# The order of 32 experts, made on the chip: the two with fewest tokens among the first 128 take the last two places

## The chip, the cores and the metric

The kernel runs on one core of a Trainium2 chip. The metric is device time in microseconds (us), from a launch to its end; lower is better. Engines are named as in the profile: PE is TensorE, DVE VectorE, ACT ScalarE, POOL GpSimd, SP SyncE, the queue that issues most DMAs.

## What is computed

The program computes one layer of a streaming encoder on 512 frames of width 1024, in float32: a norm, attention and a gated DeltaNet side by side, an output projection with a residual, and then a mixture of experts. The change is in the last part. Cut to what matters:

```python
logits = (ht @ router_w) + router_b              # 512 x 32
top_val, top_idx = lax.top_k(logits, TOP_K)      # TOP_K = 4
gates = softmax(top_val)
# each expert e works on the tokens that chose it:
gu  = xb @ w_gu[e] + b_gu[e]                     # 1024 x 2048
act = (clip(gu[:, D_FF:]) + 1) * gate * sigmoid(gate * ALPHA)
yb  = act @ w_down[e] + b_down[e]                # 1024 x 1024
y[token] += yb * gate_of_token
```

Which expert comes first is free, as each adds its part to the output. On these inputs the router of the reference gives the 32 experts this many tokens of all 512, in order of expert: 51 74 60 71 53 46 70 62 83 62 78 78 51 97 91 80 72 31 69 65 77 52 44 38 54 50 73 106 40 44 66 60. Among the first 128 tokens alone: 8 13 14 24 17 11 26 16 19 16 18 17 14 24 26 22 13 10 13 23 16 13 10 11 11 14 11 25 4 13 21 19.

## The kernel before

Everything up to the router runs in the first 340 us. Then the kernel makes lists: the tokens of each expert are cut into blocks of up to 32 (`BT`), an expert with 33 to 64 tokens has two blocks, and all blocks are numbered through. The counts above give 81 blocks; the experts 0 to 31 have 2 3 2 3 2 2 3 2 3 2 3 3 2 4 3 3 3 1 3 3 3 2 2 2 2 2 3 4 2 2 3 2 of them. `LASTB[e]` is the number of expert e's last block. Before the change expert e is worked on at position e.

Weights are loaded whole, 12 MB per expert in six transfers of 2 MB: four for gate and up (`gu_part`, L215), two for down (`dn_part`, L221), and then two small ones for the biases (`biases`, L208 and L210). There are two buffers, `GUW` and `DNW` with index 0 and 1, for even and odd positions. The experts of positions 0 and 1 are loaded early; from position 2 on the loop `reload` on SP does it. SP takes its orders strictly in turn:

- gate-up part q of position p waits (L215) until the last block of position p-2 has read part q of that buffer;
- the down parts wait (L221) for the last block's down product of p-2, which PE does after the first gate-up of position p-1;
- the biases wait for `y_free` (L208), which DVE gives in the first block of position p-1, after its own biases have arrived.

For each block PE does gate-up (L1001, 64 matmul records in the trace) and then down (L1014) of the block before. DVE adds the bias (L1386), clamps, transposes the next block's tokens into `XT` (L1377), and so on. POOL gathers the tokens of a block from memory by indirect DMA (L394; its queue is q0) and adds each finished block to the output (L409). The gather of a block starts when the block before it has been transposed, so there is one in flight. PE's next gate-up needs `XT`. At the first block of a position DVE first waits for the position's biases (L1401), and the transpose of the second block stands behind that wait.

The router: for each of four tiles of 128 tokens, `top4(t)` on DVE (L1306 to L1314) finds the four largest logits and makes the one-hot table `OH` and the counts per token `MASK`. It is put between the additions of the output projection (L1321, two for each tile, numbered n = 0 to 7 here), and PE runs projection, transposes and logits of neighbouring tiles in between (L636, L924). `COUNT` (L636) sums the masks over all 512 tokens; from it come the lists.

Of the kernel before, what the change touches and what calls it, by code (L numbers as in the profile page):

```python
# [36 lines left out]
def hybrid_block(nc, x, norm_mix_w, w_in, qn_w, kn_w, sinks, conv_w, a_log, dt_bias, out_norm_w, w_out,  # L37
                 norm_ffn_w, router_w, router_b, w_gu, b_gu, w_dn, b_dn, out):
    ctx = ExitStack()
    with ctx:  # L40
# [3 lines left out]
        def S_(name):  # L44
            if name not in sems:
                sems[name] = ctx.enter_context(nc.semaphore(name))
            return sems[name]
# [21 lines left out]
        def small(at, n):  # L69
            return SM[:, at:at + n]  # L70
# [92 lines left out]
        NBI = RT[:, 1388:1420].bitcast(I32)  # L163
        GSUM, GREC = RT[:, 1420:1424], RT[:, 1424:1428]
# [19 lines left out]
        COUNT = PS[7][:, 0:NE]  # L184
# [21 lines left out]
        def _(sp):  # L206
# [95 lines left out]
            def reload(e, p):  # L302
                through = sp.value_load(LASTB[0:1, bass.ds(e - 2, 1)], min_val=0, max_val=MAXB - 1) + 1
                gu_part(e, p, range(4), through)
                dn_part(e, p, range(2), through)
                sp.wait_ge(S_("y_free"), e - 1)
                biases(e, p)
# [7 lines left out]
        def _(g):  # L315
# [64 lines left out]
            g.wait_ge(S_("mask"), 2)  # L380
            g.tensor_tensor(MSUM[:, 0, :], MASK[:, 0, :], MASK[:, 1, :], ALU.add).then_inc(S_("msum"), 1)
            normed_out(3)
            g.wait_ge(S_("mask"), 3)
# [250 lines left out]
        def _(pe):  # L634
            def mm(o, l, r, st, sp_):
                return pe.matmul(o, l, r, start=st, stop=sp_)  # L636
# [296 lines left out]
            for n in range(2 * NT):  # L933
                t, half = n // 2, n % 2
                if half == 0:
                    pe.wait_ge(S_("dcat"), t + 1)
                if n == 0:
                    pe.wait_ge(S_("wo_in"), 16 * 3)
                    pe.wait_ge(S_("h_att"), 2 * NT)
                if n >= 2:  # L940
                    pe.wait_ge(S_("h_add"), n - 1)
                for k in range(4, KD):
                    last = mm(PS[n % 2], CAT[:, k, t * P:(t + 1) * P], WO1[:, k - 4, half * 512:half * 512 + 512], k == 4, k == KD - 1)
                last.then_inc(S_("outproj"), 1)
                if n < NT - 1:
                    dcat(n + 1)
                if n in (3, 4, 6):
                    h_transposes(n // 2 - 1)
                if n == 4:
                    pe.wait_ge(S_("rw_scaled"), 1)  # L950
                    logits(0)
                if n == 5:
                    logits(1)
# [17 lines left out]
            pe.wait_ge(S_("mask"), NT)  # L971
# [77 lines left out]
        def _(v):  # L1049
# [254 lines left out]
            def top4(t):  # L1304
                v.wait_ge(S_("lg_ps"), t + 1)
                stt(out=LG[:, t, :], in0=LGP[t % 2], scalar=RSH[:, t:t + 1], in1=RB, op0=ALU.mult, op1=ALU.add).then_inc(S_("logits"), 1)  # L1306
                v.wait_ge(S_("logits"), t + 1)
                link(v.max(MX8[:, t, :], LG[:, t, :]))
                link(v.max_index(MI8[:, t, :], MX8[:, t, :], LG[:, t, :]))
                link(v.tensor_copy(MIF[:, t, :], MI8[:, t, :]))  # L1310
                ts(GATE[:, 4 * t:4 * t + 4], MX8[:, t, 0:4], MX8[:, t, 0:1], None, ALU.subtract).then_inc(S_("v_gate"), 1)
                v.wait_ge(S_("consts"), 8)
                link(tt(OH[:, t], bm(IO32, TOPK), bc(MIF[:, t, 0:TOPK], NE), ALU.is_equal))
                v.tensor_reduce(MASK[:, t, :], OH[:, t].rearrange("p k e -> p e k"), AX.X, ALU.add).then_inc(S_("mask"), 1)  # L1314
            def normed(t):
                stt(out=HN[t], in0=H[t], scalar=RSH[:, t:t + 1], in1=FW, op0=ALU.mult, op1=ALU.mult).then_inc(S_("hn_ready"), 1)
            for t in range(NT):
                for half in range(2):
# [3 lines left out]
                    if half == 0 and t >= 2:  # L1322
                        top4(t - 2)
                    if half == 0 and t == 3:
# [13 lines left out]
            v.wait_ge(S_("count_ps"), 1)  # L1338
# [7 lines left out]
            v.wait_ge(S_("mask"), NT)  # L1346
# [108 lines left out]
```

## Time and profile before

| | |
|---|---|
| median of 3 runs | 1371.28 us (1369.92 to 1372.37) |
| the profiled execution: its time, its span | 1371.59 us, 1369.8 us |
| mean granted TensorE clock | 0.943 of full speed |
| PE busy | 1210.8 us, 88% of the span |
| DVE, POOL, ACT busy | 504.8, 283.8, 206.3 us |
| weight queue (q1) | 424.97 MB, 75.1% of 16 engines' span |
| gathers and scatters (q0) | 18.91 MB, 6.1% |

The span is cut into 40 slices of 34 us, counted here from 0. The row for DMA has the mean busy share of the 16 DMA engines in tenths, the row for GB/s what they moved. From slice 10 on, where the experts begin, the DMA engines are at 9 in all but one slice, while PE moves between 7 and 9. So neither is the only bound: which of the two waits for the other changes along the way, and the averages don't tell it. Times below are in us from the start of the span.

### The profile page before, as it was taken

How to read it: one execution, taken by the hardware profiler on the slowest of the kernel's cores; microseconds unless marked ns; L12 is line 12 of the kernel's file. 1: busy time of each engine (PE TensorE's matmuls, PEld its weight loads, DVE VectorE, ACT ScalarE, POOL GpSimd, SP SyncE). 2: the span in 40 equal slices, each digit the busy share in tenths (PEclk: the TensorE clock that was granted, in tenths of full speed). 3: DMA queues.
4: the chain of work that ended last, by engine and by line, in shares of the span. 5: the costliest groups of instructions: out<-in, count | busy, mean ns of one | idle time of the engine just before them, and what ended most of it. 6: DMA issues, size and time to landing. Idle time of an engine off the chain costs nothing.

```text
span 1369.8 us, 30476 instructions
## 1 busy us (share of the span) xinstructions
PE 1210.8 (88%) x12030; PEld 566.0 (41%) x12031; DVE 504.8 (37%) x1213; ACT 206.3 (15%) x415; POOL 283.8 (21%) x381
## 2 busy tenths in 40 slices
PE   7989997989889887979798899988989777799896
PEld 6865554766533332324233333333333222233333
DVE  1236857455333332323233233323333223233332
ACT  4135662133000000000000000000000000000000
POOL 1000004000122222223122223222222222222222
PEclk9999999899799999989899999999999988999999
DMA  6221140439789999999999999999999999998991
GB/s 204 64 67 62 31 123 8 152 147 397 312 346 415 418 419 415 417 419 416 416 417 419 399 381 395 406 403 417 417 421 418 416 421 419 421 415 353 421 408 27
DMA packets 67696, 446.55 MB, mean 326 GB/s; under 512 B 17008, under 2 KB 37688, under 8 KB 43088
## 3 DMA queue, kind: packets, MB, share of 16 engines
q1 hardware_dynamic: 48736, 424.97, 75.1%
q0 software_dynamic: 16176, 18.91, 6.1%
q10 hardware_dynamic: 2752, 2.23, 0.5%
q8 instruction: 22, 0.36, 0.1%
q14 instruction: 10, 0.08, 0.0%
HBM read 435.37 MB, written 15.07 MB: 329 GB/s over the span
## 4 chain that ended last, share of the span: by engine, by line
DMA 46%; PE 37%; DVE 7%; issue 5%; ACT 1%; POOL 1%; SPq 1%; DVEq 1%; POOLq 1%; ACTq 0%
DMA XG<-hn_scratch,IDXC 22%; DMA BDN<-in_expert_b_down 21%; PE PS L636 17%; PE PS L1001 12%; PE PS L1014 4%; DMA out<-Y,IDXS 3%; PE PSC L636 2%; DVE XT L1377 2%; POOL IDXC L391 1%; DVE GU L1386 1%; DMA W<-in_w_in 1%; SPq L208 1%; DVEq L1423 0%; DVE W L1230 0%; DVE W L1231 0%
## 5 line engine op out<-in xcount | busy, mean ns | idle before, releaser
L1001 PE MATMUL PS<-W,XT 128*32 128x512 f32 x5184 | 608.6, 623 | 116.4 <-DVE XT L1377 107.1
L1001 PEld LDWEIGHTS PS<-W,XT 128*32 128x32 f32 x5184 | 169.3, 114 | 516.5 <-issue 409.0
L1014 PE MATMUL PS<-W,AT 128*32 128x256 f32 x5184 | 294.6, 379 | 1.2 <-DVE AT L1397 1.2
L636 PE MATMUL PS<-W 128*128 128x512 f32 (+7 forms) x898 | 250.2, 439 | 10.4 <-DVE W L1175 7.5
L1014 PEld LDWEIGHTS PS<-W,AT 128*32 128x32 f32 x5184 | 169.5, 110 | 145.8 <-issue 47.8
L636 PEld LDWEIGHTS PS<-W 128*128 128x128 f32 (+1 forms) x898 | 151.8, 195 | 95.0 <-issue 75.3
L1386 DVE TENSOR_TENSOR GU<-PS,BGU 128x512 f32<-128x512 f32 x81 | 56.0, 692 | 363.1 <-PE PS L1001 360.4
L409 POOL DMA_INDIRECT out<-Y,IDXS x81 | 130.4, 1610 | 103.5 <-ACT Y L625 96.7
L625 ACT ACTIVATE Y<-SIG,ident 128x256 f32<-128x256 f32 x81 | 41.2, 508 | 656.1 <-DMA out<-Y,IDXS 629.5
L394 POOL DMA_INDIRECT XG<-hn_scratch,IDXC x82 | 87.3, 1064 | 73.4 <-POOL IDXC L391 69.3
L405 POOL COPY IDXS<-IDX 128x1 uint32 (+1 forms) x81 | 14.8, 183 | 391.9 <-DMA out<-Y,IDXS 391.8
L1377 DVE STREAM_TRANSPOSE XT<-XG 128x256 f32<-128x256 f32 x82 | 53.0, 646 | 93.6 <-DMA XG<-hn_scratch,IDXC 93.6
L619 ACT ACTIVATE SIG<-GU 128x256 f32<-128x256 f32 x81 | 33.8, 417 | 277.9 <-DVE GU L1388 271.2
L391 POOL COPY IDXC<-IDX 128x1 uint32 (+1 forms) x82 | 30.1, 367 | 201.4 <-DVE XT L1377 187.3
L1401 DVE LOAD_MASK_SELECT BGU<-BGU x32 | 0.5, 15 | 183.7 <-DMA BDN<-in_expert_b_down 176.0
L1397 DVE STREAM_TRANSPOSE AT<-GU 128x256 f32<-128x256 f32 x81 | 53.0, 654 | 33.4 <-PE PS L1014 30.0
L636 PE MATMUL PSC<-W 128*128 128x128 f32 (+5 forms) x312 | 38.5, 294 | 6.2 <-DVE W L1274 3.2
L342 POOL TENSOR_TENSOR W<-W 128x512 f32<-128x512 f32 x4 | 5.0, 1266 | 185.0 <-ACT W L490 185.0
L636 PEld LDWEIGHTS PSC<-W 128*128 128x128 f32 (+2 forms) x312 | 36.2, 208 | 11.4 <-DVE W L1274 3.8
L1394 DVE SCALAR_TENSOR_TENSOR GU<-GU,SIG 128x256 f32<-128x256 f32 x81 | 34.5, 425 | 2.8
L1392 DVE TENSOR_TENSOR SIG<-SIG,GU 128x256 f32<-128x256 f32 x81 | 33.9, 419 | 0.0
L1406 DVE TENSOR_TENSOR SIG<-PS,BDN 128x256 f32<-128x256 f32 x81 | 31.0, 383 | 3.8 <-PE PS L1014 3.8
(254 smaller groups left out, 539.9 us busy)
## 6 DMA issues: line engine op xcount, KB each, us to landing
W<-in_expert_w_gate_up SPq DMA_DIRECT2D x128, 2048.0 KB
W<-in_expert_w_down SPq DMA_DIRECT2D x64, 2048.0 KB
W<-in_w_in SPq DMA_DIRECT2D x10, 1024.0 KB, 5.3
W<-in_x SPq DMA_DIRECT2D x8, 512.0 KB, 10.2
W<-in_w_out SPq DMA_DIRECT2D x2, 1024.0 KB, 9.7
W<-in_w_out SPq DMA_DIRECT2D x1, 2048.0 KB, 8.2
hn_scratch<-W POOLq DMA_DIRECT2D x4, 512.0 KB, 11.1
out<-W ACTq DMA_DIRECT2D x4, 512.0 KB, 11.0
```

The source lines that it names most:

```text
L391: g.tensor_copy(IDXC[:, 0:1], IDX[:, bass.ds(at, 1)]).then_inc(S_("idx_cur"), 1)
L394: g.indirect_dma_start(out=XG[:, :], out_offset=None, in_=hn_d, in_offset=bass.IndirectOffsetOnAxis(ap=IDXC[:, 0:1], axis=0), bounds_check ...
L409: g.indirect_dma_start(out=acc_d, out_offset=bass.IndirectOffsetOnAxis(ap=IDXS[:, :], axis=0), in_=Y[:, :], in_offset=None, compute_op=ALU ...
L625: a.activation(Y[:, :], SIG[:, :], ACT.Copy, scale=GATEB[:, bass.ds(at, 1)]).then_inc(S_("ys_ready"), 1)
L636: return pe.matmul(o, l, r, start=st, stop=sp_)
L1001: last = pe.matmul(GPS[32 * j:32 * j + 32, :].rearrange("p (g n) -> p g n", g=2), XT[:, 32 * k:32 * k + 32], rhs, start=(k == 0), stop=(k ...
L1014: last = pe.matmul(DPS[32 * j:32 * j + 32, :], AT[:, 32 * k:32 * k + 32], DNW[p][:, k, j * QW:(j + 1) * QW], start=(k == 0), stop=(k == KD ...
L1377: v.transpose(XTV, XGV).then_inc(S_("xt_ready"), 1)
L1386: tt(GU[:, :], GPS, BGU[p][:, :], ALU.add).then_inc(S_("gu_evac"), 1)
L1392: tt(SIG[:, :], SIG[:, :], GU[:, 0:QW], ALU.mult).then_inc(S_("glu"), 1)
L1394: stt(out=GU[:, 0:QW], in0=GU[:, QW:2 * QW], scalar=1.0, in1=SIG[:, :], op0=ALU.add, op1=ALU.mult).then_inc(S_("act_ready"), 1)
L1397: v.transpose(ATV, ACTV).then_inc(S_("at_ready"), 1)
```

## The change

On DVE, after the top four of tile 0 are known, the tokens per expert among the first 128 are summed by a small matmul (`EARLY`), and 14 short instructions find the two experts, of 2 to 31, with the smallest counts. `ORDER` starts as 0 to 31; the expert with the smallest count is swapped with what stands at position 31, the second with what stands at 30. The one-hot tables compare with `ORDER` where they compared with 0 to 31, so all lists go by positions. PE's small matmul stands inside the projection n = 5, ahead of its last quarter. SP reads `ORDER` in `reload` to know which expert's weights to load. The diff, cut to its core:

```diff
+        OHA = RT[:, 1620:1748].rearrange("p (k e) -> p k e", k=TOPK)
+        ORDERI = small(184, NE).bitcast(I32)
...
-        COUNT = PS[7][:, 0:NE]
+        COUNT, EARLY = PS[7][:, 0:NE], PS[7][:, 64:64 + NE]
...
-            def reload(e, p):
-                through = sp.value_load(LASTB[0:1, bass.ds(e - 2, 1)], min_val=0, max_val=MAXB - 1) + 1
+            def reload(at, p):
+                through = sp.value_load(LASTB[0:1, bass.ds(at - 2, 1)], min_val=0, max_val=MAXB - 1) + 1
+                e = sp.value_load(ORDERI[0:1, bass.ds(at, 1)], min_val=0, max_val=NE - 1)
                 gu_part(e, p, range(4), through)
                 dn_part(e, p, range(2), through)
-                sp.wait_ge(S_("y_free"), e - 1)
+                sp.wait_ge(S_("y_free"), at - 1)
                 biases(e, p)
...
                 for k in range(4, KD):
+                    if n == 5 and k == KD - 1:
+                        pe.wait_ge(S_("consts"), 8)
+                        pe.wait_ge(S_("mask"), 1)
+                        mm(EARLY, ONER, MASKA, True, True).then_inc(S_("count_ps"), 1)
                     last = mm(PS[n % 2], CAT[:, k, t * P:(t + 1) * P], WO1[:, k - 4, half * 512:half * 512 + 512], k == 4, k == KD - 1)
...
-                v.wait_ge(S_("consts"), 8)
-                link(tt(OH[:, t], bm(IO32, TOPK), bc(MIF[:, t, 0:TOPK], NE), ALU.is_equal))
-                v.tensor_reduce(MASK[:, t, :], OH[:, t].rearrange("p k e -> p e k"), AX.X, ALU.add).then_inc(S_("mask"), 1)
+                if t:
+                    chosen(t)
+            def chosen(t):
+                link(tt(OH[:, t], bm(ORDER, TOPK), bc(MIF[:, t, 0:TOPK], NE), ALU.is_equal))
+                v.tensor_reduce(MASK[:, t, :], OH[:, t].rearrange("p k e -> p e k"), AX.X, ALU.add).then_inc(S_("mask"), 1)
+            def order_of_experts():
+                v.wait_ge(S_("consts"), 8)
+                link(tt(OHA, bm(IO32, TOPK), bc(MIF[:, 0, 0:TOPK], NE), ALU.is_equal))
+                v.tensor_reduce(MASKA, OHA.rearrange("p k e -> p e k"), AX.X, ALU.add).then_inc(S_("mask"), 1)
+                v.wait_ge(S_("count_ps"), 1)
+                link(ts(KEY, EARLY, -1.0, None, ALU.mult))
+                link(v.max(K8, KEY[:, 2:NE]))
+                link(v.max_index(KI8.bitcast(U32), K8, KEY[:, 2:NE]))
+                link(v.tensor_copy(FEW, KI8[:, 0:2].bitcast(U32)))
+                link(ts(FEW, FEW, 2.0, None, ALU.add))
+                link(ts(SWAP, IO32, FEW[:, 0:1], None, ALU.is_equal))
+                link(ts(SWAP[:, NE - 1:NE], SWAP[:, NE - 1:NE], -1.0, None, ALU.add))
+                link(ts(AWAY, FEW[:, 0:1], -1.0, float(NE - 1), ALU.mult, ALU.add))
+                link(stt(out=ORDER, in0=SWAP, scalar=AWAY, in1=IO32, op0=ALU.mult, op1=ALU.add))
+                link(ts(SWAP, ORDER, FEW[:, 1:2], None, ALU.is_equal))
+                link(ts(SWAP[:, NE - 2:NE - 1], SWAP[:, NE - 2:NE - 1], -1.0, None, ALU.add))
+                link(tt(AWAY, ORDER[:, NE - 2:NE - 1], FEW[:, 1:2], ALU.subtract))
+                link(stt(out=ORDER, in0=SWAP, scalar=AWAY, in1=ORDER, op0=ALU.mult, op1=ALU.add))
+                link(v.tensor_copy(ORDERI, ORDER))
+                chosen(0)
...
                     if half == 0 and t >= 2:
                         top4(t - 2)
+                    if half == 0 and t == 2:
+                        order_of_experts()
```

Other waits on `mask` and `count_ps` go up by one. On PE, in the projection of tiles 2 and 3, before (`PS1` is where n = 5 is summed, `PS7` where counts are):

```order
L636 MATMUL PSC<-W0,W1 128x32 x8
L636 MATMUL PS1<-W1 128x512 x4
L636 MATMUL PSC<-W0,W1 128x32 x8
L636 MATMUL PS0<-W1 128x512 x4
L924 MATMUL PS2<-ident,W1 128x128 x4
```

and with the change:

```order
L642 MATMUL PSC<-W0,W1 128x32 x8
L642 MATMUL PS1<-W1 128x512 x3
L642 MATMUL PS7<-W0 128x32
L642 MATMUL PS1<-W1 128x512
L642 MATMUL PSC<-W0,W1 128x32 x8
L642 MATMUL PS0<-W1 128x512 x4
L930 MATMUL PS2<-ident,W1 128x128 x4
```

The small matmul has come between the third and the fourth quarter of n = 5. On DVE, from the top four of tile 0 to the addition of n = 5 (`PS1`), before:

```order
L1310 CAST W0<-W0 128x8
L1311 TENSOR_SCALAR GATE<-W0 128x4
L1313 TENSOR_TENSOR W0<-W0 128x128
L1314 TENSOR_REDUCE W0<-W0 128x32
L1321 TENSOR_TENSOR W1<-W1,PS1 128x512
```

and with the change:

```order
L1329 TENSOR_TENSOR W0<-W0 128x128
L1330 TENSOR_REDUCE W0<-W0 128x32
L1332 TENSOR_SCALAR W0<-PS7 128x32
L1333 MAX W0<-W0 128x8
L1334 MAX_INDEX W0<-W0 128x8
L1335 CAST W0<-W0 128x2
...
L1344 SCALAR_TENSOR_TENSOR W0<-W0 128x32
L1345 CAST SM<-W0 128x32
L1325 TENSOR_TENSOR W0<-W0 128x128
L1326 TENSOR_REDUCE W0<-W0 128x32
L1353 TENSOR_TENSOR W1<-W1,PS1 128x512
```

Sixteen instructions now stand ahead of that addition, and the first of the 14, L1332, reads what PE has just counted. On SP, at the head of `reload`, before (`TENSOR_LOAD` reads a number into a register):

```order
L303 TENSOR_LOAD LASTB
L303 ISA x2
L214 REGISTER_ALU
L215 ISA
L215 DMA W<-in_expert_w_gate_up 128x4096
```

and with the change, where `SM` holds `ORDERI`:

```order
L308 TENSOR_LOAD LASTB
L308 ISA x2
L309 ISA
L309 TENSOR_LOAD SM
L309 ISA x2
L219 REGISTER_ALU
L220 ISA
L220 DMA W<-in_expert_w_gate_up 128x4096
```

A second load stands ahead of the first weight transfer of each position.

## Rows read from the trace of the kernel before

**Rows 1.** The page: GB/s in 40 slices; the queue of gathers and scatters.

```profile
GB/s 204 64 67 62 31 123 8 152 147 397 312 346 415 418 419 415 417 419 416 416 417 419 399 381 395 406 403 417 417 421 418 416 421 419 421 415 353 421 408 27
...
q0 software_dynamic: 16176, 18.91, 6.1%
```

**Rows 2.** Stretches: length, busy of five engines, PE clock, DMA share, GB/s.

```profile
890.00:895.00 5.00, 5.00 (x52) 1.49 (x48) 0.39 (x2) 0.51 (x1) 1.09 (x2) 1.00 0.91 326
...
1310.00:1315.00 5.00, 3.87 (x20) 0.99 (x24) 2.94 (x9) 0.42 (x1) 1.37 (x2) 0.52 1.04 421
...
1335.00:1340.00 5.00, 5.00 (x48) 1.74 (x47) 1.67 (x5) 0.00 (x0) 1.78 (x3) 1.00 0.44 114
...
895.00:1230.00 335.00, 285.94 (x3304) 107.37 (x3300) 102.96 (x263) 23.54 (x51) 82.02 (x103) 0.92 1.02 419
```

**Rows 3.** Timeline of PE, gate-up of positions 14 to 17: start, duration, work.

```profile
799.71 7.04 PE L1001 MATMUL PS<-W,XT 128*32 128x512 f32 x64
...
822.80 7.07 PE L1001 MATMUL PS<-W,XT 128*32 128x512 f32 x64 [2.04 <-DVE XT L1377]
...
833.53 7.08 PE L1001 MATMUL PS<-W,XT 128*32 128x512 f32 x64 [0.20 <-issue]
...
865.84 7.07 PE L1001 MATMUL PS<-W,XT 128*32 128x512 f32 x64 [0.17 <-DVE XT L1377]
...
888.48 7.07 PE L1001 MATMUL PS<-W,XT 128*32 128x512 f32 x64 [1.79 <-DVE XT L1377]
...
899.24 7.07 PE L1001 MATMUL PS<-W,XT 128*32 128x512 f32 x64 [0.24 <-issue]
```

**Rows 4.** Timeline of SP: weight and bias transfers issued for positions 18 and 31.

```profile
890.62 5.46 SPq L215 DMA_DIRECT2D W<-in_expert_w_gate_up  x4
...
1314.05 0.55 SPq L210 DMA_DIRECT2D BDN<-in_expert_b_down  x1
```

**Rows 5.** Timeline of PE: last quarter of gate-up of positions 18 and 24.

```profile
915.39 1.92 PE L1001 MATMUL PS<-W,XT 128*32 128x512 f32 x16 [0.19 <-DMA W<-in_expert_w_gate_up]
...
1107.06 1.92 PE L1001 MATMUL PS<-W,XT 128*32 128x512 f32 x16 [1.73 <-DMA W<-in_expert_w_gate_up]
```

**Rows 6.** Timeline of PE and DVE: position 30's second block, then position 31.

```profile
1311.13 9.97 PE L1001 MATMUL PS<-W,XT 128*32 128x512 f32 x64 [3.18 <-DVE XT L1377]
...
1345.18 7.08 PE L1001 MATMUL PS<-W,XT 128*32 128x512 f32 x64
...
1339.38 0.01 DVE L1401 LOAD_MASK_SELECT BGU<-BGU  x1 [3.05 <-DMA BDN<-in_expert_b_down]
...
1342.08 0.69 DVE L1386 TENSOR_TENSOR GU<-PS,BGU 128x512 f32<-128x512 f32 x1 [1.58 <-PE PS L1001]
...
1343.04 0.64 DVE L1377 STREAM_TRANSPOSE XT<-XG 128x256 f32<-128x256 f32 x1
```

**Rows 7.** Timeline of PE, gate-up of positions 20 to 22, six blocks apart.

```profile
985.00 8.77 PE L1001 MATMUL PS<-W,XT 128*32 128x512 f32 x64 [2.07 <-DVE XT L1377]
...
1059.35 7.07 PE L1001 MATMUL PS<-W,XT 128*32 128x512 f32 x64
```

**Rows 8.** Timeline of PE and DVE in the router's stage.

```profile
319.33 3.68 PE L636 MATMUL PS<-W 128*128 128x512 f32 x8
...
336.04 1.97 PE L636 MATMUL PSC<-W 128*128 128x32 f32 x16 [0.45 <-ACT W L606]
...
323.05 0.69 DVE L1321 TENSOR_TENSOR W<-W,PS 128x512 f32<-128x512 f32 x1 [1.66 <-PE PS L636]
...
328.27 0.69 DVE L1321 TENSOR_TENSOR W<-W,PS 128x512 f32<-128x512 f32 x1 [1.34 <-PE PS L636]
...
331.19 0.15 DVE L1328 CAST W<-W 128x1 f32<-128x1 int32 x1
331.38 0.15 DVE L1329 TENSOR_SCALAR W<-W 128x1 f32<-128x1 f32 x1
...
332.65 0.69 DVE L1321 TENSOR_TENSOR W<-W,PS 128x512 f32<-128x512 f32 x1 [1.12 <-PE PS L636]
```

More of the change, by code:

```diff
@@ L163, in hybrid_block @@
         NBI = RT[:, 1388:1420].bitcast(I32)
+        OHA = RT[:, 1620:1748].rearrange("p (k e) -> p k e", k=TOPK)
+        MASKA = RT[:, 1556:1588]
+        KEY, K8, KI8, FEW = RT[:, 672:704], RT[:, 704:712], RT[:, 712:720], RT[:, 720:722]
+        SWAP, AWAY, ORDER = RT[:, 724:756], RT[:, 756:757], RT[:, 764:796]
+        ORDERI = small(184, NE).bitcast(I32)
         GSUM, GREC = RT[:, 1420:1424], RT[:, 1424:1428]
@@ L379, in _ @@
             normed_out(2)
-            g.wait_ge(S_("mask"), 2)
+            g.wait_ge(S_("mask"), 3)
             g.tensor_tensor(MSUM[:, 0, :], MASK[:, 0, :], MASK[:, 1, :], ALU.add).then_inc(S_("msum"), 1)
             normed_out(3)
-            g.wait_ge(S_("mask"), 3)
+            g.wait_ge(S_("mask"), 4)
             g.wait_ge(S_("msum"), 1)
@@ L970, in _ @@
             mm(RANKS[:, 3, :], ONER, MSUM[:, 1, :], True, False)
-            pe.wait_ge(S_("mask"), NT)
+            pe.wait_ge(S_("mask"), NT + 1)
             mm(COUNT, ONER, MASK[:, 3, :], False, True).then_inc(S_("count_ps"), 1)
@@ L1337, in _ @@
             top4(3)
-            v.wait_ge(S_("count_ps"), 1)
+            v.wait_ge(S_("count_ps"), 2)
             link(ts(NBI, COUNT, float(BT - 1), None, ALU.add))
@@ L1345, in _ @@
             link(stt(out=BASE, in0=bm(BSF, NT), scalar=float(BT), in1=RANKS, op0=ALU.mult, op1=ALU.add))
-            v.wait_ge(S_("mask"), NT)
+            v.wait_ge(S_("mask"), NT + 1)
             link(tt(OHB, OH, BASE.rearrange("p t (o e) -> p t o e", o=1).to_broadcast([P, NT, TOPK, NE]), ALU.mult))
```

## The prediction, made before the changed kernel had run

> **What bounds the kernel now.** Start with the GB/s by slices. From slice 12 on, counted from 0, they stand at 415 to 421, but for the end and two dips: slices 22 to 26 (381 to 406) and slice 36 (353) [rows 1]. A stretch of 335 us holds 419 GB/s throughout [rows 2]. I take 419 as what the queue of weights gives when it always has work. Where it is lower, the DMA engines had nothing to move, since SP may not yet overwrite a buffer that PE still reads. So almost everywhere the next weights are the bound, and in the dips PE is.
>
> Next, put the blocks of each position beside the dips. Slices 22 to 26 are positions 13 to 17, with 4, 3, 3, 3 and 1 blocks; slice 36 is position 27, with 4. In the timeline of PE, gate-up of positions 14, 15, 16 and 17 starts at 799.71, 833.53, 865.84 and 899.24 [rows 3]: 33.8, 32.3 and 33.4 us, mean 33.2, for three blocks. What does one position cost the DMA queue? The last quarter of the gate-up weights lets PE go on at 915.39 for position 18 and at 1107.06 for position 24 [rows 5]: 191.67 us for six positions with no dip in between, 31.9 each. So three blocks in a row cost PE 1.3 us more than the weights cost the queue. Whoever has three blocks again and again falls behind; whoever has one or two lets PE catch up. Position 17, with one block, is such a rest.
>
> Last, the end. DVE gets the biases of position 31 at 1339.38; they stand in the queue behind all weights, issued at 1314.05 [rows 4, 6], and the queue falls to 114 GB/s in 1335 to 1340 [rows 2]. After the two shuffles DVE is free at 1340.50 and then waits only 1.58 us for PE's gate-up [rows 6]. So at the end too the weights and PE arrive nearly together: PE's three blocks of position 30 cost at most those 1.6 us.
>
> **What the order becomes.** Of the counts among the first 128 tokens, experts 2 to 31, the smallest is 4 (expert 28), the next 10 (experts 17 and 22, a tie). The search for an index should give the first of equals, 17. Position 31 gets expert 28, position 28 expert 31; position 30 gets expert 17, position 17 expert 30. In blocks: position 28 has two before and after, position 31 has two before and after, position 30 has one in place of three, **position 17 has three in place of one**. The total stays 81. So the last position gains nothing; the change moves two blocks from 30 to 17.
>
> **The stretch from 17 on.** Positions 14 to 20 now have three blocks each, without the rest. The queue had just run dry at the issue for position 18: issued at 890.62, 326 GB/s in that window [rows 2, 4]. The states at 865.84 and 899.24 are alike, so I let PE go on at the mean: position 20 starts at 899.24 + 3 x 33.18 = 998.8. Its third block starts 22.64 later, as in position 16 (888.48 less 865.84), at 1021.4. SP issued the weights of position 18 2.14 after the start of 16's last block, and they were in 24.77 after that (915.39 less 890.62), with an empty queue. So those of position 22 are in at 1021.4 + 2.1 + 24.8 = 1048.3. Before, with the queue always busy, they were in at about 915.39 + 4 x 31.95 = 1043.2. **Loss: 5.1 us.** With the shortest of the three position times (32.31) it is 2.5, with the longest and the longer offset of position 14 (33.82, 23.09) 7.5. From 21 on there are two blocks a position, PE catches up by about 23, and the queue never makes up what it lost; the dip at position 27 comes again, as long as before.
>
> **The end.** In position 30 there are two blocks less to gather and scatter while the last weights come. q0 moved 18.91 MB in 163 transfers [rows 1], 0.116 MB each; four of them at 419 GB/s are **-1.1 us** (by the share of time, 6.1%, it would be -2.1). Then: PE has no third block, so the first gate-up of position 31 is done before the biases come. DVE starts L1386 at 1340.50 in place of 1342.08, and `XT` is ready 1.60 later (1343.68 less 1342.08) [rows 6]: PE starts the last gate-up at 1342.1 and not at 1345.18. But it has stood still since its down product, about 9 us, and after a wait of only 3.18 us the row at 1311.13 took 9.97 in place of 7.07, in a window with 0.52 of the full clock (the 1.2 GHz level) [rows 2, 6]. So it ends between 1352.1 (at 9.97) and 1349.2 (at 7.08), against 1352.3 before. Every long wait for `XT` in this trace is followed by the slow form, so I take a little less than the upper end: **-0.5 us**, bounds -3.1 and -0.2.
>
> **The router's stage.** PE: one small matmul inside n = 5. A logits group of eight such, 16 records, takes 1.97 [rows 8], so 0.25. It stands at 319.5 + 0.75 x 3.5 = 322.1, and its result is there at about 322.4; DVE's mask is ready before that. DVE: 14 short instructions. Two neighbours stand 0.19 apart [rows 8]; ten of them at 0.20, and the two of 128x32 with three inputs, the maximum and the index at about 0.25 each make 3.0. Then the two of `chosen(0)`, 0.7. So the addition of n = 5 starts at about 326.1, not at 323.05: 3.05 late. Queued behind it on DVE are the norm of tile 2, the addition of n = 6, the top four of tile 1 and the addition of n = 7. Between them DVE waited 1.34 and 1.12 for PE [rows 8], which covers 2.46. The addition of n = 7 comes 0.6 late. From there ACT squares, copies the transposes, and PE's last logits wait for ACT (0.45 at 336.04) [rows 8]: nothing else covers it. **+0.6 us**, bounds 0.25 (PE's part alone) and 1.5. That delay reaches the end, as all later dips begin with PE.
>
> SP loads one more number for each position. Where SP waits for PE, the load is done before the wait ends. Where it doesn't, it runs ahead of a full queue: the last biases were issued at 1314.05 and in at 1339.38 [rows 4, 6], 25 us later, all of it the weights ahead of them. I take 0. The Trainium skill, "DMA: Bandwidth & Descriptors", section "Latency and other measured facts", puts a `tensor_load` at no less than about 600 ns; if each of 30 stood on the path, that would be an estimated 18 us more. The trace speaks against the path, not against the price: no row here shows the load by itself.
>
> **Sum.** Against the profiled execution's 1371.6: 5.1 - 1.1 - 0.5 + 0.6 = +4.1, so 1375.7; that execution lies 0.3 above the median, so **1375.4** against 1371.3. Forecast: slower by 0.3%. Its own bounds: 2.5 - 2.1 - 3.1 + 0.25 = -2.5, and 7.5 - 1.1 - 0.2 + 1.5 = +7.7.
>
> **The rivals.**
>
> *No loss at 17.* PE goes through 17 to 20 at the shortest pace seen, 32.3: loss 2.5, sum +1.5, 1372.8. For it: one position in three did. Against it: two didn't.
>
> *Faster.* Loss near zero, the last gate-up at the full clock (-3.1), lighter traffic (-2.1), the router +0.6: 2.5 - 5.2 + 0.6 = -2.1, and -3.6 if the loss is 1: 1367.7. It decides at 31.9 us per three-block position. Against it: 33.2 measured, and no block after a long wait ran at 7.07.
>
> *The slow pace.* Between 985.00 and 1059.35 six blocks took 12.4 each [rows 7], since the gather came late, while in positions 14 to 16 it was 11.1. There the queue of weights was long. If the gather is late whenever weights are moving at all, positions 17 to 20 go at 12.4: 11 blocks are 136.3, position 22's weights are in at 899.24 + 136.3 + 26.9 = 1062.4, loss 19.2, time 1389.5. The rows of 14 to 16, with weights moving nine tenths of the time, say no. The Trainium skill, "DMA: Bandwidth & Descriptors", section "Queues, rings and completion order", has each DMA engine take turns between its queues, packet by packet: by that rule the length of the weight queue shouldn't matter to a gather, only whether there is one. A mixture, some blocks slow, gives 1378 to 1382.
>
> *Another order.* If the tie goes to expert 22, position 17 keeps one block, position 22 has three, 30 has two. Position 22 is followed by positions of two blocks, and in 23 PE waits for its biases, so the third block is covered: 0.6 - 0.6 + a part of the end, 1371 to 1372.
>
> **How the numbers follow.** A measurement of this kernel tells about 0.2%, 2.7 us. Forecast, at 1374 to 1379: 0.52. No loss, 1371 to 1374: 0.22. Slow pace, whole or in part: 0.12. Faster: 0.09. Another order: 0.05. Slower by over 0.2%, above 1374.0: 0.48 of the forecast and 0.12, 0.60. Faster, below 1368.5: 0.09. Same: 0.31. The range 1370.5 to 1381.0 leaves out the faster case and the worse part of the slow pace.
>
> **What would show it.** Gate-up of PE in position 17 in three blocks and in position 30 in one. GB/s lower than 419 in four windows between 920 and 1030, each just ahead of a weight issue, together worth 5 us. The last quarter of position 24's weights at about 1113 in place of 1107.06. At the end: the biases of position 31 about 4.6 late, at 1344, and a gate-up behind them of 9 to 10 us. The addition of n = 7 at 333.2. It would be wrong if windows up to 1030 held 419, or if the end took less than 28 us from the arrival of the biases (30.4 before).

## The result and the profile after

| | before | after |
|---|---|---|
| median | 1371.01 us (20 runs) | 1373.73 us (20 runs, 1371.02 to 1376.02) |
| profiled execution, its span | 1371.59, 1369.8 us | 1372.61, 1370.7 us |
| mean granted TensorE clock | 0.943 | 0.946 |

The ratio is 1.0019, 95% interval 1.0012 to 1.0026: slower by 2.7 us. The forecast was 1375.4, slower by 4.1. The sign held, the time lay inside the range, and the size came out at two thirds, right at the 0.2% that a measurement tells. The median lies 0.3 us under 1374, so in the band that the prediction gave to its rival of a smaller loss at 17 (1371 to 1374, 0.22) and just outside its own (1374 to 1379, 0.52). The profiled execution of after lies 1.1 us under its median, that of before 0.6 over its own, so the two traces differ by only 0.9 in span; they show where time went, not how much in all. The page of after: GB/s by slices and the queue of gathers (compare [rows 1]), and the chain that ended last, where gathers (`XG`) had 22% and gate-up on PE 12% before:

```profile
GB/s 195 61 79 62 31 116 15 151 148 394 298 361 414 416 419 415 417 421 414 416 417 418 400 382 390 412 398 406 398 417 417 416 421 420 420 417 378 418 418 25
...
q0 software_dynamic: 16176, 18.91, 6.0%
...
DMA XG<-hn_scratch,IDXC 26%; DMA BDN<-in_expert_b_down 21%; PE PS L642 16%; PE PS L1011 10%; PE PS L1024 3%; DVE XT L1411 3%; PE PSC L642 2%; POOL IDXC L397 1%; DVE GU L1420 1%; DMA W<-in_w_in 1%; SPq L213 1%; DVE W L1240 0%; DVEq L1457 0%;
```

Slices 26, 27 and 28 stand at 398, 406 and 398 (403, 417 and 417 before). The dip of slice 36 (353 before) now falls mostly into slice 35 and is shallower (378). The gathers move the same bytes. By stretches (length, busy of five engines, PE clock, DMA share, GB/s), against the 419 throughout in [rows 2]:

```profile
920.00:925.00 5.00, 4.74 (x44) 1.46 (x48) 2.11 (x6) 0.00 (x0) 2.44 (x3) 1.00 1.01 350
...
955.00:960.00 5.00, 5.00 (x52) 1.46 (x48) 0.08 (x1) 0.51 (x1) 0.91 (x2) 1.00 0.97 366
...
985.00:990.00 5.00, 3.35 (x32) 1.07 (x36) 2.72 (x6) 0.31 (x1) 3.09 (x3) 1.00 0.87 325
990.00:995.00 5.00, 5.00 (x64) 1.95 (x60) 0.98 (x2) 0.58 (x2) 1.79 (x2) 1.00 0.87 360
920.00:1030.00 110.00, 105.91 (x1296) 42.14 (x1300) 41.04 (x102) 9.24 (x20) 33.20 (x42) 1.00 1.00 404
1030.00:1230.00 200.00, 166.40 (x1912) 61.66 (x1908) 58.85 (x153) 13.87 (x30) 47.93 (x61) 0.91 1.02 418
```

PE is busy 105.91 of 110 us up to 1030, at full clock, and the queue is not full (404 GB/s, 418 before): in this stretch PE is now the bound. The starts of gate-up on PE in positions 17 to 20, the last being the third block of 20, and SP's issues for positions 18, 22 and 29:

```profile
898.90 7.07 PE L1011 MATMUL PS<-W,XT 128*32 128x512 f32 x64 [0.20 <-issue]
...
932.01 7.07 PE L1011 MATMUL PS<-W,XT 128*32 128x512 f32 x64 [1.22 <-DVE XT L1411]
...
963.87 7.07 PE L1011 MATMUL PS<-W,XT 128*32 128x512 f32 x64 [0.18 <-issue]
...
997.00 7.05 PE L1011 MATMUL PS<-W,XT 128*32 128x512 f32 x64
...
1017.77 7.07 PE L1011 MATMUL PS<-W,XT 128*32 128x512 f32 x64
```

```profile
890.31 5.46 SPq L220 DMA_DIRECT2D W<-in_expert_w_gate_up  x4
...
1019.91 5.46 SPq L220 DMA_DIRECT2D W<-in_expert_w_gate_up  x4
...
1242.24 5.46 SPq L220 DMA_DIRECT2D W<-in_expert_w_gate_up  x4
```

Position 17 has its three blocks (898.90, and two more before 932.01). In position 24 ([rows 5]: there the last quarter let PE go on at 1107.06) PE no longer waits for this quarter:

```profile
1102.60 7.24 PE L1011 MATMUL PS<-W,XT 128*32 128x512 f32 x64
```

The router's stage: on DVE the first and last of the 14 new instructions and the additions n = 5 and n = 7, and PE's last logits (answers [rows 8]):

```profile
322.50 0.19 DVE L1332 TENSOR_SCALAR W<-PS 128x32 f32<-128x32 f32 x1 [0.95 <-PE PS L642]
...
325.54 0.18 DVE L1345 CAST SM<-W 128x32 int32<-128x32 f32 x1
...
326.38 0.68 DVE L1353 TENSOR_TENSOR W<-W,PS 128x512 f32<-128x512 f32 x1
...
333.45 0.69 DVE L1353 TENSOR_TENSOR W<-W,PS 128x512 f32<-128x512 f32 x1
...
336.84 1.97 PE L642 MATMUL PSC<-W 128*128 128x32 f32 x16 [0.86 <-ACT W L612]
```

The new work delays n = 5 by 3.3 us, n = 7 by 0.8 and the last logits by 0.8. And the end (answers [rows 6]): on PE the single block of position 30, the first quarter of position 31 and its last gate-up; on DVE the last biases.

```profile
1299.40 8.77 PE L1011 MATMUL PS<-W,XT 128*32 128x512 f32 x64 [2.39 <-DVE XT L1411]
...
1315.60 1.92 PE L1011 MATMUL PS<-W,XT 128*32 128x512 f32 x16 [3.98 <-DMA W<-in_expert_w_gate_up]
...
1344.93 8.42 PE L1011 MATMUL PS<-W,XT 128*32 128x512 f32 x64 [6.88 <-DVE XT L1411]
...
1342.01 0.01 DVE L1435 LOAD_MASK_SELECT BGU<-BGU  x1 [26.02 <-DMA BDN<-in_expert_b_down]
```

DVE has stood idle 26 us when the biases come (3.05 before): the two blocks taken from position 30 are gone from PE's end, and little is gained, since the weights and biases come no sooner.

**The sum of the two traces.** The cleanest ruler for the stretch is the time between two issues on SP, that for position 18 and that for position 29, as both stand at waits for PE on either side of it.

| | issue for 18 | issue for 29 | between | biases of 31 | blocks in 17, 30 |
|---|---|---|---|---|---|
| before | 890.62 | 1239.97 | 349.35 | 1339.38 | 1, 3 |
| after | 890.31 | 1242.24 | 351.93 | 1342.01 | 3, 1 |
| e1_same_order | 890.96 | 1240.16 | 349.20 | 1341.22 | 1, 3 |
| e2_only_28_31 | 892.23 | 1241.17 | 348.94 | 1341.74 | 1, 3 |
| e3_only_17_30 | 889.57 | 1241.90 | 352.33 | 1341.64 | 3, 1 |
| e4_17_last | 893.02 | 1244.70 | 351.68 | 1345.32 | 2, 3 |
| e5_22_30 | 888.93 | 1238.82 | 349.89 | 1339.56 | 1, 2 |

After against before: -0.3 at the issue for 18, +2.6 between the issues, +0.4 from there to the biases, and from the biases to the end of the span 28.7 in place of 30.4, so -1.7. Together +0.9 to +1.0. (The five experiments are those below.) A second ruler agrees: DVE got the biases of positions 22 to 31 2.3 to 3.1 later than before (at position 24, 1119.13 against 1116.85).

### The profile page after: what moved, and what is told of

Its sections match the earlier page's. It is cut to its first block, busy times and chain, and to the rows that moved or that the text cites. A ratio compares the mean times of both kernels' runs of the same rounds, so it can differ in the third digit from the quotient of the medians.

```text
span 1370.7 us, 30618 instructions
## 1 busy us (share of the span) xinstructions
PE 1206.7 (88%) x12032; PEld 564.9 (41%) x12033; DVE 508.4 (37%) x1230; ACT 206.3 (15%) x415; POOL 284.4 (21%) x381
## 4 chain that ended last, share of the span: by engine, by line
DMA 48%; PE 34%; DVE 8%; issue 5%; POOL 1%; ACT 1%; SPq 1%; POOLq 1%; DVEq 1%; ACTq 0%
DMA XG<-hn_scratch,IDXC 26%; DMA BDN<-in_expert_b_down 21%; PE PS L642 16%; PE PS L1011 10%; PE PS L1024 3%; DVE XT L1411 3%; PE PSC L642 2%; POOL IDXC L397 1%; DVE GU L1420 1%; DMA W<-in_w_in 1%; SPq L213 1%; DVE W L1240 0%; DVEq L1457 0%; DVE W L1241 0%; DVE BDN L1436 0%
## 6 DMA issues: line engine op xcount, KB each, us to landing
W<-in_x SPq DMA_DIRECT2D x8, 512.0 KB, 10.1
hn_scratch<-W POOLq DMA_DIRECT2D x4, 512.0 KB, 10.1
```

## The experiments

The medians of before in the four batches were 1371.01 to 1371.42, and each ratio below is against runs of before on the same chip. A ratio needn't be that of the two medians; a difference of 1 us is within what either can tell. Theory A: the loss comes of position 17's three blocks. Rival B: it comes of the added instructions. Rival C: of the swap of experts 28 and 31, or of their place in memory.

**The change without any new order.** In after, the sum that turns the two found indices into experts is given fixed experts; every instruction of the change stays.

```diff
-                link(ts(FEW, FEW, 2.0, None, ALU.add))
+                link(ts(FEW, IO32[:, 30:32], -1.0, 61.0, ALU.mult, ALU.add))
```

> All instructions of the change stay, but the two numbers that say whom to swap are 31 and 30, so the order comes out as 0 to 31. Theory A (the rest at position 17 is what is lost): only the router's stage is left, +0.3 to +0.9 us against the kernel before, 1371.5; the weights of position 18 at the same place as before and no window under 400 GB/s between 895 and 1230. Theory B (the added instructions cost it: the small matmul, 14 short ones on DVE, the second load of SP for each position): the whole difference, +2.5 us or more.

1371.27 us (11 runs), ratio 1.0008 (0.9999 to 1.0017), +1.1 us by the ratio and nothing by the medians (1371.31 before). Its stretch up to 1030 is full again:

```profile
920.00:1030.00 110.00, 96.29 (x1173) 37.68 (x1168) 36.79 (x93) 8.30 (x18) 28.40 (x36) 0.97 1.02 418
```

The added instructions, SP's loads among them, cost 1.1 us by this, not clear of nothing, and no more than 2.3 by the interval. Rival B wanted 2.5 or more and a loss without a new order: by the times it is only just excluded, by the full queue up to 1030 plainly, as far as the dip goes.

**Only experts 28 and 31 swapped, only 17 and 30 swapped.** The same line with `IO32[:, 28:30], 2.0, -28.0`, and with `IO32[:, 1:3], -14.0, 45.0`.

> As the first, but expert 28 and expert 31 are swapped (both have two blocks). Theory A: the same time as with the order unchanged, within 0.7 us. Theory B: +2.5 us. A third, C (it matters from which addresses the last weights come): differs from the unchanged order by more than 1.5 us, in the last 40 us.

> As the first, but only experts 17 and 30 are swapped. Theory A: the same as the full change, +2.7 us against the kernel before (1373.7), with windows under 380 GB/s near 955 and 990 and the biases of position 31 at 1341.5 to 1343. Theory B: no more than with the order unchanged.

Only 28 and 31: 1372.40 (12 runs), ratio 1.0005 (0.9995 to 1.0015), no more than e1, and 418 GB/s up to 1030. Only 17 and 30: 1375.50 (5 runs; 1373.7 was expected), ratio **1.0038** (1.0025 to 1.0051). Here, in order, the stretch, PE's last gate-up and DVE's last biases:

```profile
920.00:1030.00 110.00, 106.43 (x1300) 42.28 (x1304) 42.08 (x103) 9.25 (x20) 35.04 (x43) 1.00 1.00 403
```

```profile
1344.57 8.46 PE L1011 MATMUL PS<-W,XT 128*32 128x512 f32 x64 [5.03 <-DVE XT L1411]
...
1341.64 0.01 DVE L1435 LOAD_MASK_SELECT BGU<-BGU  x1 [26.22 <-DMA BDN<-in_expert_b_down]
```

It is after's picture line for line: 403 GB/s, the biases after 26 us of idleness, a gate-up of 8.5. Between the issues for 18 and 29 it lost 3.0 us on before and 3.1 on e1 (table above). So theory A holds for the dip, and C falls for experts 28 and 31. That its ratio lies above that of the whole change, with intervals that barely touch, I can't explain; five runs are few, and the profiled execution, 1372.51, is the fastest of them, so that its trace doesn't show the other 3 us.

**Position 30 shortened, but the rest kept.** Expert 22 (2 blocks) goes to position 30, expert 30 (3) to position 22, and 28 and 31 are swapped as in the change: `IO32[:, 0:2], -6.0, 28.0`.

> All instructions of the change stay; 28 and 31 are swapped and then 22 and 30, so position 22 has three blocks for two, position 30 two for three, and position 17 keeps its rest. Theory A (the rest at 17 is what is lost): within 1 us of the kernel with the order unchanged, 1371.3 to 1372.4, no window under 400 GB/s between 895 and 1230. Rival (a shorter position 30 makes the end longer, since PE cools down while it waits for the last weights): 1374 to 1375, as with the full change.

1373.25 (11 runs), ratio 1.0014 (1.0005 to 1.0023). That is between theory A (1371.3 to 1372.4) and the rival (1374 to 1375), and its interval holds both e1 and after, so the time alone doesn't decide. The trace does for the dip: between the issues it took 349.89 us, within 0.7 of e1, with 418 GB/s up to 1030. The biases came at 1339.56, and yet it was no faster than e1, since PE stood still ahead of the last gate-up:

```profile
1342.47 9.48 PE L1011 MATMUL PS<-W,XT 128*32 128x512 f32 x64 [8.72 <-DVE XT L1411]
```

From the biases to the end of that gate-up e5 takes 12.4 us, e1 10.1: e1 still had a block of position 30 to do, so PE was busy up to it, and its gate-up ran in 7.07. So e5 gave back there (2.3) the 1.7 by which its biases came earlier; 2.0 of lead it had already at the issue for 18, which is scatter and not the order. From the biases to the end of the span, three blocks in position 30 took 30.4, 27.7 and 29.6 us (before, e1, e2), two took 29.9 (e5), one took 28.7 and 29.0 (after, e3): what is saved by shortening position 30 is no larger than the scatter between executions. Its blocks are nearly free: they hide behind the last weights, and where they were missing the last gate-up ran in 8.42 to 9.48 in place of 7.07.

**The one-block expert last.** If position 30 hides, position 31 should not: every block of it stands behind the biases. `IO32[:, 0:2], 13.0, 17.0` puts expert 17 at position 31 and expert 31 (2 blocks) at position 17.

> As the first, but expert 17 (one block) goes to position 31, and expert 31 (two blocks) to position 17. Theory A: position 17 with two blocks still lets PE catch up (two blocks cost 22.1 us, the weights 31.9), so no dip between 895 and 1230; position 31 has one block, so its second gate-up and down are gone from the end: the stretch from the arrival of the last biases to the end shrinks from 30.4 to 19 to 21 us, total about 1361. If the end is instead set by a chain of scatters or of gathers, the gain is 5 us or less.

1364.18 (6 runs), ratio 0.9952 (0.9934 to 0.9970), **7.1 us under before by the medians**, some 3 us short of what I expected. The end is what was expected: the span ends 18.1 us after the biases, where before it was 30.4. But the biases came 5.9 later (1345.32 against 1339.38): 2.4 of it stood already at the issue for 18, and 2.3 is a dip that I had excluded, as position 17 still had a short rest of two blocks. On PE the starts of position 18's first two blocks and of 19's first, then the window at the end of position 20, then DVE's last biases:

```profile
924.38 7.07 PE L1011 MATMUL PS<-W,XT 128*32 128x512 f32 x64 [1.89 <-DVE XT L1411]
936.88 7.07 PE L1011 MATMUL PS<-W,XT 128*32 128x512 f32 x64 [1.97 <-DVE XT L1411]
...
962.25 8.77 PE L1011 MATMUL PS<-W,XT 128*32 128x512 f32 x64 [2.84 <-DVE XT L1411]
```

```profile
1020.00:1025.00 5.00, 4.57 (x28) 1.29 (x32) 2.27 (x6) 0.51 (x1) 2.29 (x4) 0.66 0.70 239
```

```profile
1345.32 0.01 DVE L1435 LOAD_MASK_SELECT BGU<-BGU  x1 [3.95 <-DMA BDN<-in_expert_b_down]
```

The two-block rest had let the queue fill up: the weights of position 19 were issued at 917.11, while the biases of 18, ahead of them in the queue, came in only at 928.17. Position 18's blocks then came 12.5 us apart (924.38 to 936.88, and 37.9 for three, 924.38 to 962.25), each waiting 1.5 to 2 us for `XT`. That is the slow pace of [rows 7]. With PE slower, the queue ran dry at the end of position 20 (239 GB/s); it lost 4.2 us by the mean of 402 GB/s over 920 to 1030, and 2.3 by the time between the two issues (351.68). So two blocks at position 17 cost nearly as much as three, by another way. The slow pace, a rival in the prediction, is real, and my reading is that a backlog in the queue of weights brings it on; no run varies that by itself. The changed kernel doesn't meet it in positions 17 to 20, but does right behind them: 1038.93, 1051.69, 1064.58, 1077.15, 12.6 to 12.9 apart.

**The last position chosen from all 512 tokens.** Built on before: no early count. Behind `COUNT`, short instructions on DVE find the expert with the fewest blocks, exchange it with position 31 in the block counts and starts, and write `ORDERI`; PE's filler behind the ranks grows from 16 to 27.

```diff
-            link(v.tensor_tensor_scan(BEF, ONE32, NBF, 0.0, ALU.mult, ALU.add))
-            link(tt(BSF, BEF, NBF, ALU.subtract))
+            link(ts(KEY, NBF, -1.0, None, ALU.mult))
+            link(v.max(K8, KEY[:, 2:NE]))
+            link(v.max_index(KI8.bitcast(U32), K8, KEY[:, 2:NE]))
...
+            link(tt(D1, NBF[:, NE - 1:NE], K8[:, 0:1], ALU.add))
+            link(stt(out=NBP, in0=SWAP, scalar=D1, in1=NBF, op0=ALU.mult, op1=ALU.add))
+            link(v.tensor_tensor_scan(BEF, ONE32, NBP, 0.0, ALU.mult, ALU.add))
...
+            link(stt(out=ORDER, in0=SWAP, scalar=AWAY, in1=IO32, op0=ALU.mult, op1=ALU.add))
```

> A version for use: no count of the first 128; when the tokens of all 512 are counted, the expert of 2 to 31 with the fewest blocks (17) is swapped with the one at position 31. 12 short instructions more on DVE's path from the count to the lists, +2.4 us before the experts start; the start of experts may hide a part. The end as in the run with 17 last, -12.3 us; the weight queue loses some 4 us between 920 and 1030 as there. Sum 1364 to 1366 against 1371.3.

**1362.10** (6 runs), ratio 0.9943 (0.9928 to 0.9958): the lowest median of the study, 9 us under before and 2 under the 1364 to 1366 expected. The order is that of e4, and the intervals of the two overlap. The last gate-up on PE and the last down, and the biases on DVE:

```profile
1335.72 7.07 PE L1007 MATMUL PS<-W,XT 128*32 128x512 f32 x64 [2.07 <-DVE XT L1398]
...
1347.42 3.66 PE L1020 MATMUL PS<-W,AT 128*32 128x256 f32 x64 [1.17 <-DVE SIG L1427]
...
1341.20 0.01 DVE L1422 LOAD_MASK_SELECT BGU<-BGU  x1 [3.76 <-DMA BDN<-in_expert_b_down]
```

Gate-up of the only block is done by 1342.8, 1.6 after the biases, and only down products follow. The count of all tokens sees what the first 128 don't: expert 17 ties with 22 at 10 there, and has 31 against 44 in all, one block.

**Long and short experts in turn.** If rests are what counts, an order in which three- and two-block experts alternate should leave no dip at all. A table fixed in the program, written by POOL, takes the place of what was computed: 0 1 2 3 4 6 5 8 7 10 9 11 12 13 21 14 15 17 16 22 18 23 19 24 20 25 26 28 27 29 30 31, and a second one with 17 last: 0 1 2 3 4 6 5 8 7 10 9 11 12 13 21 14 15 22 16 23 18 24 19 25 20 28 26 29 27 31 30 17.

```diff
+                v.wait_ge(S_("table"), NE)
+                link(v.tensor_copy(ORDER, TAB))
                 link(v.tensor_copy(ORDERI, ORDER))
```

> The order is a fixed table, put into memory by GpSimd ahead of the router: from position 2 on experts with two blocks and with three or four in turn, 17 in the middle at position 17, expert 31 (two blocks) last as in the kernel before. Theory A: no run of three-block positions, so the windows between 780 and 900 and at 1230 to 1245 that were under 400 GB/s stay at 415 or more; what they lost, about 8 and 5 us, comes back: 1358 to 1361. If the dips have another cause (a slower stretch of memory, the gathers), 1370 or more.

> As the alternating table, but expert 17 with its one block at position 31. Theory A: both gains add up, 1346 to 1350. If PE is late at position 30 (three blocks ahead of the last) the gain at the end is only 8 us, 1350 to 1353.

Both miss widely. Alternating: **1378.21** (5 runs), ratio 1.0045 (1.0031 to 1.0059), where 1358 to 1361 was expected. With 17 last: 1368.70 (12 runs), ratio 0.9977 (0.9966 to 0.9988), 4 to 7 us slower than e4 and e6, where 1346 to 1350 was expected. In the alternating order two stretches at the four-block experts (positions 13 and 28), then PE's last two gate-ups:

```profile
790.00:795.00 5.00, 5.00 (x84) 2.40 (x80) 3.21 (x8) 0.42 (x1) 1.38 (x2) 1.00 0.56 207
...
1270.00:1275.00 5.00, 5.00 (x76) 2.06 (x72) 2.70 (x7) 0.42 (x1) 1.38 (x2) 1.00 0.33 118
```

```profile
1342.27 7.07 PE L1014 MATMUL PS<-W,XT 128*32 128x512 f32 x64 [2.06 <-DVE XT L1416]
1352.59 7.08 PE L1014 MATMUL PS<-W,XT 128*32 128x512 f32 x64
```

The small dips of positions 14 to 17 did vanish, but they were never the large ones. Those stand at the experts with four blocks, whatever comes before. My reading, which the move of the biases below supports: SP may write to a buffer only when the last of its blocks has been through gate-up, and the first of them can't be finished until its biases have come, which stand behind 12 MB in the queue; from there four blocks last longer than what is queued. And the second four-block expert now stands at 28, with three blocks in 30, so that PE itself is late at the end: its last gate-up comes at 1352.59 and not at 1345.18, and that accounts for the 7.3 us between the profiled executions (1378.86 and 1371.59). The biases of position 31 came without a wait, at 1344.14, as in the second order (its row on DVE):

```profile
1344.50 0.01 DVE L1440 LOAD_MASK_SELECT BGU<-BGU  x1
```

I had judged the end by the weights alone. Part of e7's loss was there from the start: PE's first gate-up at 363.33 (361.64 in after), position 2 at 421.27 (417.59 in after). Why, I don't know.

**Biases ahead of the down weights.** If the late biases hold the first block, issue them earlier. On SP, in before:

```diff
                 gu_part(e, p, range(4), through)
-                dn_part(e, p, range(2), through)
                 sp.wait_ge(S_("y_free"), e - 1)
                 biases(e, p)
+                dn_part(e, p, range(2), through)
```

> The kernel before with one thing moved: SP issues a position's biases ahead of its two down transfers, not behind them, so they arrive some 10 us earlier. Theory D (what ties PE to the end of the queue are the biases, so that a four-block position always drains the queue, and the last position always starts as late): the first block of a position is activated 10 us earlier, the dips at 785 to 795 and 1230 to 1245 (4.5 and 5.4 us) shrink to under 2 us together, and the end from the last weights on gets shorter: 1350 to 1358 against 1371.4. Rival (the dips come from PE's own pace alone): 1366 or more.

> The changed kernel with the same move. Theory D: position 30's one block now counts, since the end hangs on PE's last blocks and the down weights, not on the biases; the sign of the change turns: 2 to 6 us faster than the kernel before with the move. Rival (what is lost at position 17 stays the larger part): slower than the kernel before with the move by 1 to 4 us.

> The version that puts the expert with the fewest blocks of all 512 tokens last, with the same move. If the two gains add up: 8 to 10 us faster than the kernel before with the move, 1341 to 1349. If the end is now set by the down weights of the last position, which arrive at the same time whatever it holds, less: 3 to 6 us.

| with the move | median | ratio to before | without the move |
|---|---|---|---|
| before | 1370.41 (11 runs) | 1.0001 (0.9992 to 1.0011) | 1 |
| after | 1369.05 (11 runs) | 0.9990 (0.9982 to 0.9999) | 1.0019 |
| 17 last, chosen from all | 1363.04 (6 runs) | 0.9945 (0.9933 to 0.9957) | 0.9943 |

In before it changes nothing, where 1350 to 1358 was expected, and in the fastest kernel nothing either (1341 to 1349 expected; it lies 7.4 under before with the move, between the 8 to 10 and the 3 to 6 of the two theories). After with the move lies 1.4 under before with the move, where theory D wanted 2 to 6 and the rival 1 to 4 the other way: neither came. The stretches of before with the move, then PE's and DVE's rows at its end:

```profile
780.00:800.00 20.00, 16.55 (x192) 6.20 (x188) 7.05 (x18) 1.85 (x4) 6.33 (x8) 0.93 1.00 408
800.00:895.00 95.00, 89.84 (x1072) 34.97 (x1068) 30.11 (x75) 7.91 (x17) 25.20 (x33) 0.98 0.98 387
...
1250.00:1330.00 80.00, 67.96 (x848) 26.96 (x838) 24.78 (x62) 6.47 (x14) 19.38 (x25) 1.00 1.00 406
```

```profile
1330.62 7.07 PE L1001 MATMUL PS<-W,XT 128*32 128x512 f32 x64 [2.13 <-DVE XT L1377]
...
1332.49 0.01 DVE L1401 LOAD_MASK_SELECT BGU<-BGU  x1
```

Without the move these stretches stood at 330, 399 and 418 GB/s. So the deep dip went (408; in 1230 to 1250, too, 399 in place of 308), as it should if the late biases hold the first of four blocks, and a good part of it came back spread over the stretches behind it (387, 406). The biases are there early now, at 1332.49 without a wait; in their place each gate-up waits some 2 us for `XT`, so for its gather. That with one gather in flight PE has no slack to win back is my reading; no run here has two. With the move, though, after is no longer slower than before (1369.05 against 1370.41, a difference of 0.1% whose intervals overlap): the price of the change may hang on the place of the biases, too. Between the issues for 18 and 29 the two differ by only 0.7 us (344.11 and 344.76), where without the move it was 2.6, though up to 1030 the queue still falls to 408 GB/s against 418. In before with the move, the biases no longer wait for anything and PE sets the end, so the blocks of position 30 aren't hidden any more; in after with the move they are gone, and DVE waits again:

```profile
1334.91 0.01 DVE L1435 LOAD_MASK_SELECT BGU<-BGU  x1 [23.32 <-DMA BDN<-in_expert_b_down]
```

That fits, but the last gate-up comes at 1341.32 and 1341.77 in the two, so there is at most half a microsecond in it, and two runs are no proof.

## The prediction, step by step

The mechanism and the sign were right, and the number was helped by luck: the largest term was nearly twice too large, and errors of other terms and of the two profiled executions made up for part of it.

- **The order**: as computed, tie to expert 17, three blocks in position 17, one in 30, two in 28 and 31.
- **The loss at 17**: right in mechanism and sign (e3 has it, e1, e2 and e5 don't), and the term that was mis-sized: 5.1 forecast, **2.6** measured between the two issues (3.0 in e3), at the very edge of my bounds of 2.5 to 7.5. Two numbers failed in it. Positions 17 to 20 went at 32.7 us each (997.00 less 898.90, by three) and not 33.2; and the third block of 20 came 20.8 after the first (1017.77 less 997.00), not 22.6. So the weights of position 22 were issued at 1019.91, 3.6 before my 1023.5. I had taken the offset of one position as that of all; where no block waits for `XT`, two blocks take 20.8. Other rulers agree on the order of size: 404 in place of 418 GB/s over the 110 us to 1030 is 3.7 us. Three stretches fell to 325 to 366 GB/s there, not four. And the dip at position 27 did not come again as long as before: 1230 to 1250 held 354 GB/s, 308 before.
- **Position 24's last quarter at 1113**: wrong as put. PE reached it with its weights already there (1102.60, 64 records without a wait), so by about 1108. The queue was late all the same, by half of what I forecast: DVE waited for the position's biases until 1119.13 (1116.85 before), and PE's second block followed at 1122.04 (1119.89 before). PE's wait for one quarter was no good mark, as PE comes late itself.
- **Lighter traffic at the end, -1.1**: not settled. From the issue for 29 to the biases, one block in position 30 took 99.8 and 99.7 us (after, e3), three took 99.4 in before but 101.1, 100.6, 100.6 and 100.4 in e1, e2, e4 and e6. By the means it is -0.7, against before alone +0.4. The biases of 31 came 2.6 late, at 1342.01, and not 4.6.
- **The last gate-up, -0.5**: sign right, size low. It ran in 8.42 after 6.88 us of waiting, between the 7.08 and 9.97 that I had and under the 9 to 10 that I named as a sign; from the biases to the end that makes -1.7 (28.7 for 30.4). But e1 and e2, with three blocks in position 30, took 27.7 and 29.6, so that a good part of it is scatter. The choice "a little less than the upper end" rested on one row with half the full clock; e5 shows that 9.48 was as possible.
- **The router, +0.6**: n = 5 at 326.38 (forecast 326.1), n = 7 at 333.45 (333.2), last logits +0.8. The first gate-up of the experts was 2.4 late (361.64, 359.24), yet the second block of position 1 only 0.5 at 396.95 (396.45), as the gate-ups between ran shorter (7.07 for 8.06, 8.77 for 9.48). e1 measures all the added instructions at +1.1, with -0.1 to 2.3.
- **SP's second load, 0**: inside e1's 1.1. The Trainium skill, "DMA: Bandwidth & Descriptors", section "Latency and other measured facts", gives such a load at least about 600 ns, an estimated 18 us for 30 in a row on the path; e1 excludes that they stand on the path. The load by itself shows in no run here.
- **Rivals**: what I called no loss at 17 was in its sum a small one: a pace of 32.3 per position, loss 2.5, 1372.8. Measured are 32.7, 2.6 and 1373.73, so this rival came nearer than the forecast, in the term and in the time (0.9 off, mine 1.7); e3 refutes its name, not its sum. The slow pace doesn't come in positions 17 to 20 of the changed kernel. Faster and another order did not come: the tie went to 17.

Against the profiled execution the forecast was 3.1 us too high (+4.1, measured +1.0), term by term: the loss 2.5 too large, the end 1.2 too dear, the router 0.9 too dear (-0.3 at the issue for 18, by a mark that scatters), and against these 1.5 for traffic (-1.1 forecast, +0.4 found). By the medians it was only 1.7 too high, as after's profiled execution lies 1.1 under its median. In the table of the kernel before, the DMA engines are said to be at 9 tenths from slice 10 on; it is from slice 12, as slices 10 and 11 are lower (312 and 346 GB/s in [rows 1]); what they lose is no part of this study.

## What to carry to other kernels

When weights stream through two buffers at the bandwidth of memory, find out which pieces of work lie behind the last transfer: only those are on the path, here the blocks of the last position (12 us of the tail went with one block, e4; e4, e6 and e11 all gained 0.5 to 0.6%), while shortening the one before it saved nothing clear of the scatter. Ahead of the end, don't take a short position out of a run of long ones to shorten something that is hidden: two blocks put there cost 2.6 to 3.0 us, one cost 2.3 (e4). But rests spread evenly are no cure by themselves: the alternating order was 6 us slower than before; its large dips stood at the four-block positions as ever, and PE came late to the end. And choose by the quantity that costs time (blocks of all tokens) once it is known, not by an early sample of another.

## What the runs showed of the hardware

How long a gather takes goes with what is in the queue of weights, and so does the pace of a block. From its issue on POOL to DVE's transpose of what it brought, where DVE waited for it, a gather took 10.0 to 10.5 us in positions 18 and 19 of e4 (issued at 926.01, 938.24, 950.93 and 963.44), and blocks stood about 12.5 us apart ([rows 7], too; e4 at 924.38 and 936.88). In after, positions 17 to 20, where the weights are issued only as PE frees them, all but one (10.62) took 7.1 to 9.7, and the same work went at 32.7 for three blocks, 10.9 each. The two shortest, at 988.64 and 1019.57, took 7.15 and 7.14, and were issued just ahead of the next weights (988.79 and 1019.91). Idle DMA engines are not the reason, or not alone: in the 10 us from 1019.57 on they moved 418 GB/s. The Trainium skill, "DMA: Bandwidth & Descriptors", section "Queues, rings and completion order", has each DMA engine take turns between its queues packet by packet; by that alone a gather's time should not depend on the length of the other queue. The times here speak for a dependence; what makes it stays open.

A gate-up block of 64 records takes 7.07 us at the full clock and 8.4 to 10.0 after some waits, with a granted clock of about half in a part of it (0.52 in the window of [rows 2] at 1310, the 1.2 GHz level). How long PE stood still doesn't tell it well: after 2.39 us it was 8.77 (1299.40 in after), after 2.06 it was 7.07 (e7 at 1342.27), after 6.88 it was 8.42, after 8.72 it was 9.48 (e5). A forecast of such a block should keep both ends.

One execution against another of the same order scatters by more than the effects in question: the issue for position 18 stood at 888.93 to 893.02 in after, e1, e2, e3, e4 and e5, which do the same up to there. Differences between two marks in one trace (348.9 to 349.9 without the dip, 351.7 to 352.3 with it) told the orders apart where the marks themselves didn't.

Open are: what two gathers in flight would do to the dips (not tried), why e7's experts start later, why e3 lies above the whole change, and how a backlog of weights slows a gather.
